# Opening each feed-forward layer with two direct tiles instead of four, ahead of its seven-product pairs

## The reference

```python
def swiglu_ffn(h, w_in, w_out):
    g, u = jnp.split(h @ w_in, [D_FF], axis=-1)
    return (jax.nn.silu(g) * u) @ w_out

yp = yp + swiglu_ffn(rmsnorm(yp, norm_ffn[i]), w_ffn_in[i], w_ffn_out[i])   # the same for ys
```

## Time and profile before

| | |
|---|---|
| median of 3 runs | 1247.15 us (1246.67 to 1247.26) |
| the profiled execution | 1247.89 us, span 1246.1 us |
| TensorE busy | 1229.2 us, 9256 matmuls, mean granted clock 0.997 |
| VectorE busy | 924.5 us (74%) |
| ScalarE busy | 673.8 us (54%) |
| GpSimd busy | 375.5 us (30%) |

### The profile page before, as it was taken

How to read it: one execution, slowest core, us unless ns; L and a number is a source line. 1 busy time by engine, 2 the same in 40 slices (tenths; PEclk the granted TensorE clock), 3 DMA queues, 4 the chain that set the end, 5 groups by cost and what they waited for, 6 DMA issues and landing times.

```text
span 1246.1 us, 23998 instructions
## 1 busy us (share of the span) xinstructions
PE 1229.2 (99%) x9256; PEld 1184.6 (95%) x9256; DVE 924.5 (74%) x1710; ACT 673.8 (54%) x1285; POOL 375.5 (30%) x262
## 2 busy tenths in 40 slices
PE   8999999999999999999999999999999999999997
PEld 8988899999999999999889998899999999999997
DVE  5666757999777877668456788678998777876755
ACT  5565644477677756743022545223477577766632
POOL 1000033422222222236566444365322222222210
PEclk9999999999999999999999999999999999999998
DMA  9511112257777777733232322323267777777722
GB/s 324 173 44 52 37 67 85 69 138 158 181 162 170 159 169 161 170 110 120 69 118 72 136 92 104 106 70 117 69 159 171 161 162 168 167 166 164 162 97 77
DMA packets 58929, 160.69 MB, mean 129 GB/s; under 512 B 8016, under 2 KB 12048, under 8 KB 57376
## 3 DMA queue, kind: packets, MB, share of 16 engines
q1 hardware_dynamic: 33536, 106.71, 27.0%
q0 software_dynamic: 21312, 38.81, 19.5%
q10 hardware_dynamic: 3968, 13.64, 3.1%
HBM read 151.66 MB, written 9.44 MB: 129 GB/s over the span
## 4 chain that ended last, share of the span: by engine, by line
PE 90%; DVE 5%; issue 2%; ACT 1%; DMA 1%; SPq 0%; DVEq 0%; ACTq 0%
PE ps L730 28%; PE ps L732 27%; PE ps L731 27%; PE ps L860 1%; PE ps L883 1%; PE ps L907 1%; PE ps L1208 1%; PE ps L1215 1%; DMA wst<-w_blocks_in 1%; PE ps L1199 0%; DMA wlo<-w_blocks_in 0%; DVE more_sum L1665 0%; PE ps L1235 0%; PE ps L1223 0%; PE ps L764 0%
## 5 line engine op out<-in xcount | busy, mean ns | idle before, releaser
L681 POOL TENSOR_TENSOR wlo<-wst,whi 128x1024 fp32r<-128x1024 f32 x63 | 160.6, 2549 | 242.0 <-ACT whi L2317 239.3
L730 PE MATMUL ps<-xhi,whi 128*128 128x288 f32 x688 | 209.1, 304 | 1.1 <-DVE wlo L1429 0.7
L731 PE MATMUL ps<-xlo,whi 128*128 128x288 f32 x688 | 202.9, 295 | 0.0
L732 PE MATMUL ps<-xhi,wlo 128*128 128x288 f32 x688 | 202.2, 294 | 0.0
L690 POOL DMA_DIRECT2D wlo<-w_blocks_in x100 | 86.5, 865 | 289.6 <-ACT wlo L2398 285.7
L730 PEld LDWEIGHTS ps<-xhi,whi 128*128 128x128 f32 x688 | 129.0, 187 | 9.7 <-issue 8.5
L730 PE MATMUL ps<-thi,more_hi 128*128 128x288 f32 x432 | 128.0, 296 | 1.7 <-ACT kept L2416 1.6
L731 PEld LDWEIGHTS ps<-xlo,whi 128*128 128x128 f32 x688 | 129.3, 188 | 0.2
L732 PEld LDWEIGHTS ps<-xhi,wlo 128*128 128x128 f32 x688 | 129.5, 188 | 0.0
L730 PE MATMUL ps<-bhi,whi 128*128 128x288 f32 x432 | 128.0, 296 | 0.0
L732 PE MATMUL ps<-bhi,wlo 128*128 128x288 f32 x432 | 127.9, 296 | 0.0
(11 more groups left out here) (362 smaller groups left out, 3765.9 us busy)
## 6 DMA issues: line engine op xcount, KB each, us to landing
wst<-w_blocks_in SPq DMA_DIRECT2D x188, 512.0 KB, 3.8
wlo<-w_blocks_in POOLq DMA_DIRECT2D x100, 256.0 KB, 4.6
more_lo<-w_blocks_in POOLq DMA_DIRECT2D x48, 256.0 KB, 5.6
S<-s_in ACTq DMA_DIRECT2D x4, 1024.0 KB, 5.0
s_sample_out<-S ACTq DMA_DIRECT2D x4, 1024.0 KB, 4.7
bias<-bias_in SPq DMA_DIRECT2D x1, 2048.0 KB, 11.4
x<-x_in SPq DMA_DIRECT2D x4, 288.0 KB, 6.9
x<-x_in ACTq DMA_DIRECT2D x4, 288.0 KB, 6.0
```

What stands on the lines that cost most here:

```text
L681: nc.gpsimd.tensor_tensor(lo, wst[:, slot, :], raw(hi), ALU.subtract).then_inc(w_split, 1)
L730: mm(out, stat[0], mov[0], start=start, stop=False, skip_group_check=skip)
L731: mm(out, stat[0], mov[1], start=False, stop=False, skip_group_check=skip)
L732: return mm(out, stat[1], mov[0], start=False, stop=stop, skip_group_check=skip)
```

## The change

`N_DIRECT` goes from 4 to 2, so tiles 2 and 3 become units and `FIRST` is the unit of tile 2. GpSimd makes the lows of the first three blocks only; the fourth is made on VectorE (`block_low`), which also makes the first unit's A11 low (`first_a11_low`). The first unit's A12 and A22 come by adding DMA. In the first unit the second product is run ahead of the sixth. VectorE's and ScalarE's lists for the opening are written anew. The diff, cut to what the lists say:

```diff
-N_DIRECT = 4
+N_DIRECT = 2
 def by_transfer(q, u):
-    return u != FIRST and (q, u) != ("A22", LAST)
+    return (q, u) not in (("A11", FIRST), ("A22", LAST))
...
@@ GpSimd @@
             def ffn(l):
-                for n in range(B_F1[l], IN_AT[l][N_DIRECT]):
+                for n in range(B_F1[l], B_F1[l] + 3):
                     split(n)
-                quarter_low("A11", l, FIRST)
                 quarter_low("A12", l, FIRST)
+                quarter_low("A22", l, FIRST)
                 for u, nxt in zip(UNITS, UNITS[1:]):
                     quarter_low("A11", l, nxt)
-                    quarter_low("A22", l, u)
+                    if u != FIRST:
+                        quarter_low("A22", l, u)
                     quarter_low("A12", l, nxt)
@@ TensorE, seven @@
                     product(5, "S1", "T1", u, 7, True)
-                    if last:
+                    if last or u == FIRST:
                         product(2, "A12", "B21", u, 6, True)
@@ VectorE @@
+                def block_low(n):
+                    dve.wait_ge(act_split, NOT_OWN.index(n) + 1)
+                    dve.wait_ge(*split_of(n - 1))
+                    hi, lo = ring(n)
+                    tt(lo, wst[:, n % STAGE, :], raw(hi), ALU.subtract).then_inc(w_split, 1)
+
+                def first_a11_low(u):
+                    hi, lo, _ = quarter("A11", l)
+                    dve.wait_ge(q_hi["A11"], ordinal(l, u))
+                    tt(lo, stage(u, "11"), raw(hi), ALU.subtract).then_inc(q_lo["A11"], 1)
...
+                late = range(B_F1[l] + 3, IN_AT[l][N_DIRECT])
                 gate(0)
-                normed_x(0, 4)
+                normed_x(0, KC)
                 up(0)
-                normed_x(4, KC)
-                direct_low(0)
-                gate(1)
+                block_low(late[0])
                 dve.wait_ge(x_normed, KC * (l + 1))
                 token_sum("T1", b12, x11)
                 token_sum("T3", x22, b12)
-                up(1)
+                direct_low(0)
+                gate(1)
+                first_a11_low(first)
+                sum_s1(first)
                 dve.wait_ge(t_summed, 4 * l + 2)
                 token_sum("T2", x22, sum1)
                 dve.wait_ge(t_summed, 4 * l + 3)
                 token_sum("T4", x21, sum2)
-                direct_low(1)
-                gate(2)
                 operand_low("B11")
+                operand_low("T1")
+                sum_s2(first)
+                sum_low("S1", first)
+                up(1)
                 operand_low("B21")
-                up(2)
-                operand_low("T1")
-                sum_s1(first)
-                direct_low(2)
-                gate(3)
-                sum_s2(first)
                 operand_low("T2")
-                sum_low("S1", first)
-                operand_low("B22")
                 sum_s4(first)
                 sum_low("S2", first)
-                up(3)
+                operand_low("B22")
                 sum_s3(first)
                 sum_low("S4", first)
                 operand_low("T3")
@@ ScalarE @@
                 late_split(ahead[0])
                 silu(0)
+                operand_high("B11")
                 late_split(ahead[1])
-                half_high(0)
-                operand_high("B11")
-                late_split(ahead[2])
-                silu(1)
                 operand_high("B21")
                 operand_high("B22")
+                half_high(0)
                 operand_high("T1")
-                late_split(ahead[3])
-                half_high(1)
+                quarter_high("A11", first)
+                silu(1)
                 operand_high("T3")
+                quarter_high("S1", first)
                 operand_high("T2")
+                quarter_high("A12", first)
                 operand_high("T4")
-                late_split(ahead[4])
-                silu(2)
-                late_split(ahead[5])
-                half_high(2)
-                for q in ("A11", "A12", "S1"):
-                    quarter_high(q, first)
-                silu(3)
                 quarter_high("S2", first)
+                quarter_high("A22", first)
+                a22_negative(first)
```

More of the change, by code:

```diff
@@ L1053, in seven @@
                     product(6, "S2", "T2", u, a, False)
-                    if not last and not fresh_out:
+                    if not last and not fresh_out and u != FIRST:
                         product(2, "A12", "B21", u, 6, True)
@@ L1594, in hidden_sum @@
                     out, left, right = htraw[op][:, j, :], h32[:, 0:H], h32[:, H:N]
-                    if op == "T1" and f < N_DIRECT:
-                        dve.wait_ge(u_read[l], f + 1)
+                    if op == "T1" and f < 4:
+                        dve.wait_ge(*((u_read[l], f + 1) if f < N_DIRECT else (seven_read, ordinal(l, ("in", f)))))
                         out, a, b = early_t1[:, j, :], htraw["T3"][:, j, :], left
@@ L1832, in ffn @@
                         corner(u)
-                        direct_low(3)
+                        direct_low(N_DIRECT - 1)
                     elif fresh_out:
@@ L1865, in ffn @@
                         hidden_sum("T4", f)
-                    if u in UNITS[1:4]:
+                    if u in (("in", 5), ("in", 6), ("in", 7)):
                         early_t1_low(u[1] - 5)
@@ L1881, in ffn @@
                             sum_low("S2", nxt)
-                    if light:
+                    if light and f >= 8:
                         sum_of_hidden_low("T1", f)
@@ L2468, in ffn @@
                         late_split(n0)
-                    quarter_high("A22", u)
+                    if u != FIRST:
+                        quarter_high("A22", u)
                     if light:
@@ L2473, in ffn @@
                         hidden_high(prev[1])
-                    a22_negative(u)
+                    if u != FIRST:
+                        a22_negative(u)
                     copy(6, u)
@@ L2485, in ffn @@
                         quarter_high("A12", nxt)
-                    if u == FIRST:
+                    if u == ("in", 4):
                         early_t1_high(0, 1)
```

## The result

The changed kernel takes 1257.99 us (median of four runs, 1257.79 to 1258.93) beside 1247.20 for the kernel before; the ratio is 1.009, 95% interval 1.0078 to 1.0102. That is 10.8 us slower, against 10.6 forecast. The profiled execution took 1258.00 us, its span is 1256.1.

A forecast was written before the change was run, and what follows sets the result against it. TensorE bounds the kernel, its opening already near a VectorE bound. 6.4 us saved, 18.2 of lateness, 2.7 of copy waits, less 3.9 of old waits: 10.6 more, 1257.8 against the median (1258.5 against the profiled execution); range 1252.5 to 1263.

The forecast's parts named there:

- Matmuls: Two tiles in two layers by seven products instead of direct: 48 matmuls fewer, 9208 for 9256, 6.4 us less.
- VectorE's list in layer 0: VectorE's steps from gate(0) at 208.95 to the first pair's S3 low: 30.7 us long, first pair 9.1 us late.
- the silent rows: Trace rows of VectorE steps with GpSimd silent, used to price the list; a token sum or low 1.27 us.
- rival C: VectorE's steps in the opening are shorter than priced; list of 25.4 us equal, 21.6 gives 1238; chance 0.06 faster, 0.04 same.
- Block low: TensorE's second direct tile, second block, waits for the block low made on VectorE: starts near 218.3, 2.1 us late.
- B11's low: First pair's first product waits for this low on VectorE: about 2.5 us, starting near 227.3.
- the four of about 1: First pair's TensorE waits for the lows of S1, B21, S2 and S4 on VectorE, about 1 us each.
- the copy: Second pair's product 6 waits for ScalarE's copy: 1.35 us, starting at 247.55 where 246.2 was due.
- rival D: Waits in each opening bring TensorE's granted clock to 1.2 GHz: 8 us a layer, 1274; chance 0.03.
- The common point: Product 7 of tile 7's pair, behind which both kernels have the same lists: 5.4 us lost in layer 0, 5.2 in layer 1.
- The tie: First pair's A12 low by adding DMA: there by 232.7, product 2 due at 232.75; 0, at worst 1.5 us a layer.
- The starving: Skill's warning that GpSimd-issued DMAs starve while VectorE holds the shared port pair; forecast expected none, issues taking 0.88 us.

The follow-up runs named there:

- experiment 1: The changed kernel with the token sums T1 and T3 computed twice in each layer's opening; 1264.62 us, ratio 1.0141 to the kernel before.
- experiment 2: The changed kernel with the first pair's A12 and A22 lows subtracted on GpSimd again instead of adding DMAs; 1261.27 us, ratio 1.0113 to the kernel before.
- experiment 4: The changed kernel with the first pair's second product back behind its sixth; 1261.54 us, ratio 1.012 to the kernel before.
- experiment 8: From the changed kernel: three direct tiles, VectorE's and ScalarE's lists reordered by need, then again for waits at product 7 and a transfer; 1245.14 us, ratio 0.9984.
- experiment 6: Kernel before with the change's adding DMAs, T3 and T4 lows ahead of the first pair's S4 sum, second pair's copy ahead of A11's high; 1245.64 us.
- experiment 7: The kernel before, four direct tiles, with the sums of T1 and T3 made twice; 1252.89 us, ratio 1.0045.
- experiment 9: Experiment 6's kernel with the first pair's A22 high and negative on ScalarE ahead of its S3 high; 1244.82 us, ratio 0.9984 to the kernel before.

## Why the prediction was right, point by point

- **Matmuls.** 9208, a product step of 1.60 us: as forecast.
- **VectorE's list in layer 0.** Forecast against measured: TensorE's fourth block 218.3 and 218.18; first product 227.3 and 227.35; end of S1's low 229.80 and 229.87; product 7 at 239.8 and 239.77. The steps taken from the silent rows hold in this list, so rival C (shorter steps) falls. Experiment 1 shows the bound itself.
- **Each wait.** Block low 2.1 forecast, 1.77 and 1.20 measured; B11's low 2.5, and 1.00 and 2.50; the four of about 1 were 0.64 to 1.02; the copy 1.35, and 1.11 and 1.09. Part of the gap is how they are counted: a bracket begins where the last matmul's record ends, some 0.2 us behind its issue step. By starts the copy's product was forecast at 247.55 and came at 247.48. The short wait of 1.00 has another cause, given under rival D.
- **The common point.** Tile 7's product 7: 297.0 forecast and 297.05 measured, and in layer 1, with layer 0's loss ahead of it, 948.0 + 5.4 = 953.4 and 953.36. Against the earlier trace rows that is 5.43 and 5.14 us lost, 10.57 in all. Between the profiled executions the difference is 10.1, so about 0.5 came back outside of these stretches.
- **The transfers.** The first pair's A12 low was issued at 227.10 and landed within 4.9 us, ahead of product 2 at 232.81. The tie was won, and by experiment 2 the move is a gain of 3.3 us within this change, not the nothing at which it was put: left on GpSimd, the two lows would have lengthened the list. The starving that the prediction weighs did not come: the issues in this opening took 0.86 to 1.01 us beside a VectorE without a pause. In the Trainium skill (SBUF — State Buffer, "SBUF: two separate sides") that warning is given for VectorE operations in a two-port mode, a condition that the prediction left out; no row here tells in which mode a step ran.
- **The second product's place.** Put at nothing in itself. By its own steps that was right (235.25 for 235.43 in experiment 4), but it keeps two waits apart, behind which as one the clock fell in layer 1 of that experiment and cost 1.5 us; by the medians the order is worth 3.5 us, 2 of them unexplained. That step failed, though the total did not ask for it.
- **Rival D.** It was set aside because the longest new wait would be 2.6 us. That reason failed: the clock fell in layer 0 behind a wait of 1.77. The block from 218.18 took 8.0 us in place of 6.4, but TensorE had to wait for B11's low at its end anyway, and that wait is 1.00 there where layer 1, at full clock, has 2.50. So the fall cost nothing, by the cover of another wait. That is luck: nothing in the forecast provided for it.
- **What the change lacked.** Not fewer tiles as such: with three, the lists in another order, and the same transfers, the time is 2.1 us less than the kernel before's (experiment 8). Two tiles leave a list of 30.7 us with 20.8 us of work beside it.

## What to carry to other kernels

Before matmuls are taken away, add up the list of the engine that feeds them, step by step from the rows, and compare it with the work that is left beside it; a TensorE that is busy for all of a stretch says nothing of how near the other bound is. When the list is the bound, the gain lies in its length and order: a wait that an engine has in its own list is a place to put later steps (experiment 6), and a step that nobody awaits can go behind one that is awaited, though part of the gain may come back as the next wait (1.8 us of 3.5 were won in experiment 8). A long single wait can cost more than the same time in pieces: in experiment 4 the clock fell behind one of 3.63 us, and 1.5 us were lost, while behind one of 3.38 neither happened.

## What the runs showed of the hardware

- **The granted clock can fall behind a wait of under 2 us, and the wait's length alone does not say whether it falls.** In layer 0 of the changed kernel it was 0.70 and 0.87 behind a wait of 1.77 us; in experiment 4 it stayed at 1.00 behind the same wait of 1.77, was 0.58 behind the next, of 2.51 (the first product, at 227.17), and again 1.00 behind one of 3.38. It was 0.50 behind a wait of 3.79 (experiment 1), 0.78 and 0.80 around one of 3.63 (experiment 4, layer 1), 0.58 behind one of 1.90 (experiment 7), and 1.00 behind those of 1.20 and 2.50 in layer 1 of the changed kernel. It was 1.00 in the opening before and in experiments 8 and 9. A matmul's step at the lower level is 0.24 us here, against 0.133.
- **A low on GpSimd holds up a VectorE step with two operands in SBUF until it ends.** Steps of 1.35 and 0.75 us took 2.44 and 2.95 when they began beside one (experiments 2 and 7); steps that read one operand from PSUM kept their 0.46 and 0.45 (experiment 2). The same lows by adding DMA held nothing up: their issues took 0.87 and 1.01 us beside a VectorE without a pause.
- **A wait that the trace puts down to nothing can be a transfer.** The 0.94 us of experiment 6, marked as issue, ended 0.1 us behind the landing of a transfer (263.1), and went when that transfer was started earlier (experiment 9).
